# The prompt's second gate multiplied onto expert rows in the rounds instead of onto the final tiles

## The reference, cut to what matters

```
def run_trunk(x, c, ...):
    sh1, sc1, gt1, sh2, sc2, gt2 = jnp.split(mod[:, None, :], 6, axis=-1)
    ...
    h = rmsnorm(x, p['g_norm_ffn'][l]) * (1.0 + sc2) + sh2
    x = x + gt2 * hier_moe(h, l, p)
    ...
    y = rmsnorm(x, p['g_final'])

def hier_moe(h, l, p):      # every row goes to 2 of 32 experts
    for e in range(N_EXPERTS):
        hid = jax.nn.silu(x @ p['w_exp_gate'][l, e]) * (x @ p['w_exp_up'][l, e])
        out = out + combine[:, e:e + 1] * (hid @ p['w_exp_down'][l, e])
```

## Time and profile before

| | |
|---|---|
| median of 3 runs | 1513.41 us (1513.18 to 1515.0) |
| the profiled execution | 1518.33 us, span from first to last instruction 1516.6 us |
| busy PE, DVE, ACT, POOL | 1367.9, 532.2, 284.2, 125.8 us |
| rounds | 1147 to 1437 us of the span |
| loop, one turn | 1438 to 1457 us |
| gathers and final tiles | 1463 to 1516.6 us |
| mean granted TensorE clock | 0.949 of full speed |

### The profile page before, as it was taken

How to read it: one execution, slowest core, us unless ns; L and a number is a source line. 1 busy time by engine, 2 the same in 40 slices (tenths; PEclk the granted TensorE clock), 3 DMA queues, 4 the chain that set the end, 5 groups by cost and what they waited for, 6 DMA issues and landing times. The chain is left out here.

```text
span 1516.6 us, 20884 instructions
## 1 busy us (share of the span) xinstructions
PE 1367.9 (90%) x8687; PEld 899.4 (59%) x8687; DVE 532.2 (35%) x1186; ACT 284.2 (19%) x666; POOL 125.8 (8%) x138
## 2 busy tenths in 40 slices
PE   4999999999999999998999999999967999999830
PEld 3565667888988666665567656689853333333210
DVE  4423222224433225780290224343752421111118
ACT  4100000003433310112322212121221111111103
POOL 0000000110020015001000000000001000000033
PEclk9799999999999989999999999999977999999965
DMA  9423422323441253232410355440055999999748
GB/s 311 143 84 124 134 83 92 104 82 118 166 179 53 74 148 122 76 130 74 84 57 10 121 161 172 162 148 28 29 218 208 361 378 415 418 416 415 300 126 245
DMA packets 132895, 256.55 MB, mean 169 GB/s; under 512 B 23191, under 2 KB 97575, under 8 KB 124585
## 3 DMA queue, kind: packets, MB, share of 16 engines
q1 hardware_dynamic: 106850, 192.29, 35.9%
q0 software_dynamic: 11264, 34.23, 6.9%
q10 hardware_dynamic: 14688, 28.71, 5.1%
HBM read 207.77 MB, written 50.17 MB: 170 GB/s over the span
## 5 line engine op out<-in xcount | busy, mean ns | idle before, releaser
L380 PE MATMUL psum<-h_t,ring 128*128 128x352 f32 x576 | 174.1, 464 | 2.7 <-DVE h_t L545 2.7
L380 PEld LDWEIGHTS psum<-h_t,ring 128*128 128x128 f32 x576 | 110.1, 192 | 65.6 <-issue 6.4
L1069 PE MATMUL psum<-h_t,ring 128*128 128x352 f32 x384 | 119.3, 469 | 3.2 <-PEq L667 3.2
L2137 PE MATMUL psum<-ring,big 128*128 128x256 f32 x512 | 116.7, 387 | 2.1 <-PEq L1819 2.1
L2137 PEld LDWEIGHTS psum<-ring,big 128*128 128x128 f32 x512 | 97.9, 194 | 16.3 <-issue 3.1
L2244 PE MATMUL psum<-w_gate_up,u_rows 128*32 128x512 f32 x608 | 100.3, 601 | 2.9 <-ACT u_rows L2365 1.1
L2244 PE MATMUL psum<-ring,u_rows 128*32 128x512 f32 x576 | 100.3, 596 | 0.9 <-ACT u_rows L2365 0.9
L1069 PEld LDWEIGHTS psum<-h_t,ring 128*128 128x128 f32 x384 | 73.4, 194 | 42.9 <-issue 5.6
L395 PE MATMUL psum<-ring,h_t 128*128 128x256 f32 x384 | 92.4, 397 | 0.0
L395 PEld LDWEIGHTS psum<-ring,h_t 128*128 128x128 f32 x384 | 85.5, 285 | 3.5 <-issue 0.4
L2266 PE MATMUL psum<-big 128*32 128x512 f32 x736 | 83.7, 595 | 0.8 <-DVE big L2676 0.8
(11 more groups left out here) (462 smaller groups left out, 1862.6 us busy)
## 6 DMA issues: line engine op xcount, KB each, us to landing
big<-in_w_exp_down SPq DMA_DIRECT2D x32, 1024.0 KB, 13.1
ring<-in_w_ada SPq DMA_DIRECT2D x24, 1024.0 KB, 7.2
w_gate_up<-in_w_exp_gate SPq DMA_DIRECT2D x13, 1024.0 KB
w_gate_up<-in_w_exp_up SPq DMA_DIRECT2D x13, 1024.0 KB
ring<-in_w_exp_gate SPq DMA_DIRECT2D x13, 1024.0 KB, 6.5
ring<-in_w_exp_up SPq DMA_DIRECT2D x13, 1024.0 KB, 8.6
tmp_expert_rows<-zero_rows POOLq DMA_DIRECT2D x12, 1024.0 KB
ring<-in_w_in SPq DMA_DIRECT2D x11, 1024.0 KB, 8.5
```

The lines of the kernel that those rows point to most:

```text
L380: m = nc.tensor.matmul(bank[(e + j) % NB][:, 0:CW], w[:, k, c * P:(c + 1) * P], ht3[:, k, j * CW:(j + 1) * CW], start=(k == 0), stop=(k == ...
L1069: m = T_.matmul(bank[4 + u % 4][:, 0:CW], w_[:, k, c0:c0 + P], ht3[:, k, j * CW:(j + 1) * CW], start=(k == 0), stop=(k == KT - 1))
L2137: m = T_.matmul(bank[2 * (i % 2) + b // 2][0:r, (b % 2) * WB:(b % 2 + 1) * WB], merged_t[:, k, t * P:t * P + r], w[:, k, :], start=(k == 0 ...
```

## The change

1. `copy_down` is DVE's alone. For each half it first builds `gate_of`, 128 x 512 (`gate_rows`: the prompt's gate where the row's token is a prompt token, one elsewhere), waits for it, and multiplies the bank by it on the way to `y_e`. That is four dependent instructions instead of one, and ACT's copy is gone.
2. On DVE `copy_hid(b)` now stands ahead of `copy_down(b - 1)`.
3. PE and ACT wait for DVE's semaphore alone.
4. The loop does the same: two flags, two gate halves, and two multiplications at its end.
5. In the final tiles the multiplication by `gate2` is left for the sample tile alone.
6. Three small instructions after routing and two in `overflow_map` make the flags of every slot (1 or 0 by the token's number). A few tiles move in SBUF.

```diff
                 def store(b):
-                    act.wait_ge(s_dna, b + 1)
                     act.wait_ge(s_dnd, b + 1)
...
                     if b + 1 < ROUNDS:
                         copy_x(b + 1)
                     if b >= 1:
-                        copy_down(b - 1)
                         store(b - 1)
...
+                c.step(dve, V.tensor_copy(tok_f[:, :], tok_i[:, :]))
+                c.step(dve, V.tensor_scalar(of_prompt[:, 0:ROUNDS], tok_f[:, :], float(SEQ), None, ALU.is_lt))
+                c.step(dve, V.tensor_scalar(of_sample[:, 0:ROUNDS], of_prompt[:, 0:ROUNDS], -1.0, 1.0, ALU.mult, ALU.add))
...
                     dve.wait_ge(s_dn, b + 1)
                     if b >= 2:
                         dve.wait_ge(s_yst[b % 2], 16 * (b // 2))
-                    V.tensor_copy(y_e[b % 2][:, 512:D], bank[5]).then_inc(s_dnd, 1)
+                    for f in range(2):
+                        gate_rows(b, f)
+                        m = V.tensor_tensor(y_e[b % 2][:, 512 * f:512 * (f + 1)], bank[4 + f], gate_of[:, :], ALU.mult)
+                        if f == 0:
+                            c.step(dve, m)
+                        else:
+                            m.then_inc(s_dnd, 1)
+
+                def gate_rows(b, f):
+
+                    c.step(dve, V.scalar_tensor_tensor(out=gate_of[:, :], in0=row_p["gate2"][:, 512 * f:512 * (f + 1)], scalar=of_prompt[:, b:b + 1],
+                                                       in1=of_sample[:, b:b + 1].to_broadcast([P, 512]), op0=ALU.mult, op1=ALU.add))
...
                 for b in range(ROUNDS):
                     hidden(b)
+                    copy_hid(b)
                     if b >= 1:
                         copy_down(b - 1)
-                    copy_hid(b)
...
                 with dve.Fori(0, turns) as n:
+                    V.tensor_copy(lflag[:, 0:1], of_prompt[:, bass.ds(n + ROUNDS, 1)]).then_inc(s_llw, 1)
+                    V.tensor_copy(lflag[:, 1:2], of_sample[:, bass.ds(n + ROUNDS, 1)]).then_inc(s_llw, 1)
+                    dve.wait_ge(s_llw, 2 * n + 2)
+                    for f in range(2):
+                        V.scalar_tensor_tensor(out=gate_loop[f], in0=row_p["gate2"][:, 512 * f:512 * (f + 1)], scalar=lflag[:, 0:1],
+                                               in1=lflag[:, 1:2].to_broadcast([P, 512]), op0=ALU.mult, op1=ALU.add).then_inc(s_lgate, 1)
...
-                    V.tensor_copy(ly[:, 512:D], bank[5]).then_inc(s_ldnd, 1)
+                    V.tensor_tensor(ly[:, 0:512], bank[4], gate_loop[0], ALU.mult)
+                    V.tensor_tensor(ly[:, 512:D], bank[5], gate_loop[1], ALU.mult).then_inc(s_ldnd, 1)
...
                         dve.wait_ge(s_both[t], 16)
-                        c.step(dve, V.tensor_tensor(a, a, (row_p if t < TT else row_s)["gate2"][0:r, :], ALU.mult))
+                        if t == TT:
+                            c.step(dve, V.tensor_tensor(a, a, row_s["gate2"][0:r, :], ALU.mult))
```

## The result

Six runs of the changed kernel had a median of 1525.3 us (1523.16 to 1526.96), six of the one before 1514.2 (1511.37 to 1517.65): a ratio of 1.0062, 95% interval 1.0049 to 1.0076. So it is slower, as forecast, but 1525.3 lies outside the range of 1515.5 to 1522.0, and 11.1 us is nearly twice the +5.7 of the sum.

What follows compares the result with a forecast made beforehand. Bounds: PE and weight loads in the rounds, then last copies, loop and gathers, finally DVE with DMA nearly level. 2.63 + 2.27 + 0.61 + 1.8 - 1.6 = +5.7 us on a 1513.4 median gave 1519.1, range 1515.5 to 1522.0.

Steps and rivals of the forecast that it cites:

- The mid rounds cost nothing: Rounds before the last: the longer copy_down, 2.96 us for 0.69, fits DVE's idle time and adds nothing.
- the rival of the rounds: Rounds: later stores meet other weight loads, PE's weight waits double or triple, +3 to +5 us, about 1522.5; chance 0.10.
- The last round, +4.9: Last round: down(22) starts 2.63 us later, and the bare copy_down(22) delays PE's loop entry by 2.27.
- The loop's end, +0.61: End of the loop: two multiplications on DVE where ACT had taken one half, the second starting 0.61 us later.
- The clock, +1.8: Half clock after PE's longer gaps: down(22) +1.5 us, loop's transposes +0.8, products -0.5; between -3 and +8.
- The tail, -1.6: Final tiles: fewer DVE multiplications, but gather landings limit the gain to 1.6 us, between -0.8 and -3.7.
- The rival by which POOL's gathers come earlier: Final tiles: less DVE work lets POOL issue gathers earlier, 2.6 us back, +3.1 in all, 1516.5; chance 0.12.

Runs made afterwards that it cites:

- e1: The kernel before, unchanged, run again as a control: 1516.17 us against 1515.43, ratio 0.9994.
- e12: Changed kernel with gates built a round ahead, loop's turn count read early, final norm's row loaded by ScalarE ahead of the last store: 0.9975 of before.
- e5: Kernel before with only the order changed, copy_hid(b) ahead of copy_down(b - 1) on DVE: 1.0003 of before.
- e6: Kernel before with the final tiles' eight multiplications by the prompt's gate left out, nothing added: 0.9985 of before.
- e7: Changed kernel with unread products in PE's gaps, three ahead of down(22), three behind it, one in the loop: 1.0012 of before.
- e11: The changed kernel, unchanged, measured a third time: 1522.16 us, 1.0036 of before.
- e10: Changed kernel with gates built a round ahead from round 7 and the loop's turn count read early by PE and ScalarE: 0.998 of before.

## Why the prediction was right in direction and too small

**The mid rounds cost nothing: right.** H alone says little: it lies between 1422.8 and 1433.5 in nine profiles with the new copies in some form (mean 1429.9) and between 1428.4 and 1433.3 in five with the old ones (mean 1430.8). But the rounds themselves can be timed, from the `turn_x(1)` that ends round 0 to H. These are the rows of `turn_x(1)` in before and in the changed kernel:

```profile
1158.69 1.12 PE L2223 MATMUL psum<-ident,big 128*128 128x128 f32 x8
...
1160.74 1.12 PE L2228 MATMUL psum<-ident,big 128*128 128x128 f32 x8
```

To H it is 272.67 us in before and 272.69 in e1, and 272.80, 272.74 and 272.77 in the three profiles of the changed kernel: 0.1 us for 22 rounds. The tightest round came out a little tighter than computed, and still harmless (changed kernel, timeline; `hidden(3)` and the `turn_hid(3)` that needs it):

```profile
1194.75 0.24 DVE L2651 TENSOR_SCALAR overflow_block<-overflow_block,w_top 128x25 f32<-128x25 f32 x1
1195.20 0.48 DVE L2666 SCALAR_TENSOR_TENSOR big<-big,weight_of_slot,psum 128x256 f32<-128x256 f32 x1 [0.21 <-DVE overflow_block L2651]
...
1198.72 0.44 PE L2258 MATMUL psum<-ident,big 128*128 128x128 f32 x2
```

3.0 us to spare, where 3.2 were computed. PE's waits for gate and up weights went from 2.4 us to 2.9 in the same two places; a third wait, which the prediction left out, went from 0.8 to 0.5. So the rival of the rounds falls.

**The last round, +4.9: right.** Measured 2.72 (forecast 2.63) for `down(22)`'s start, and 2.3 to 2.5 (2.27) for the loop's entry behind the last copy.

**The loop's end, +0.61: wrong in sign.** From the last of the loop's products of gate and up to POOL's first gather it was 12.19 and 12.06 us in before and e1, and is 11.80, 11.71 and 11.85 in the three profiles of the changed kernel: -0.3. The copy is longer, as computed, but the later store meets less of the norm row's load and lands a microsecond sooner (e12). I had costed a DMA as if it were alone.

**The clock, +1.8: too small.** This is the term that was mis-sized. `down(22)` lost 2.83, 1.70 and 1.70 us (taken: 1.5, after a discount of one third for the case that the clock holds; it fell in all three profiles). The transposes lost 0.8, as taken. The products I let win 0.5 against the 10.00 of the earlier trace rows, and here it depends on what one compares with. The kernel before itself shows 10.00 and 9.97, the changed one 9.71, 9.62 and 9.62: -0.3, and the term is 2.1 + 0.8 - 0.3 = +2.6. But e5 and e6, with the old copies too, show 8.77 and 7.13; against the mean of all four, 9.0, the term is 2.1 + 0.8 + 0.7 = +3.6. Four profiles can't say which is nearer. By the rule of the Trainium skill that the prediction names ("TensorE: Matmul & The Clock Gate", Part 1, What's actually happening) each lengthened gap speaks against the change; the 0.50 in the windows above and e7 agree.

**The tail, -1.6: right.** -1.5, and its cause as well: tile 7's second gather started 27.35 us after the first one and landed 14.0 later, before 26.80 and 14.2. So the rows arrive when they did. The rival by which POOL's gathers come earlier falls with it. By line, the accumulating gathers of the changed kernel

```profile
L2126 POOL DMA_INDIRECT big<-tmp_expert_rows,slot_i x9: 1535/1590/2270, 1478.2 to 1504.8; - x9
```

and of before

```profile
L2121 POOL DMA_INDIRECT big<-tmp_expert_rows,slot_i x9: 1460/1544/2372, 1467.9 to 1493.9; - x9
```

take as long as ever, though DVE has eight instructions with two SBUF inputs less. The rule of the Trainium skill on the shared port pair ("SBUF — State Buffer", Who interferes with whom) may hold, but the removed instructions were not what made gathers long.

**The sum.** 2.7 + 2.3 - 0.3 + 2.6 - 1.5 = +5.8 us, or +6.8 with the larger clock term. The stretches after H of the three changed profiles and of before and e1 differ by 5.7 us in the mean (87.0 against 81.3), and the later comparisons gave 6.2 and 5.7. So the forecast of +5.7 was near what the change costs, with errors on both sides that partly cancelled: the loop's end 0.9 too high, the clock 0.8 or more too low.

**The first 1525.3.** It lies 6.2 us over the forecast of 1519.1. 2.4 of these are the base: three runs gave 1513.41, while the 128 later runs of the kernel before have a median of 1515.8, spread from 1505.6 to 1523.1. Another 0.4 is between the median difference of 24 later runs of the changed kernel (1521.9 - 1515.8 = 6.1) and 5.7. The remaining 3.4 lie between the first six runs of the changed kernel and these 24.

Most of that is the clock again, in a place where the sum put it at nothing. The mean granted clock was measured in every run. Over the 128 runs of before, the time falls by 1.2 us for each 0.001 of it (correlation -0.95), and over the 24 of the changed kernel by 1.1 (-0.94). The first six had a mean clock of 0.9463, the 24 one of 0.9485: 2.2 steps, about 2.5 of the 3.4 us. The profiled one of the six took 4.7 us more than that of e11, 3.2 of it in front of H and 1.5 behind. The traces say what makes H early or late. For each of the 14 profiles, take windows of 10 us from the start to H and add up (1 - clock) x length, the time that the granted clock took away. This sum runs from 34.0 us (e12, H 1422.78) to 47.8 (the changed kernel's first profile, H 1433.54), with 46.2 in before and 42.6 in e1. H follows it with a correlation of 0.99, 0.8 us for each us. One such place is round 0, here in the changed kernel and in e12:

```profile
1140.00:1160.00 20.00, 13.16 (x80) 5.51 (x80) 0.80 (x5) 2.31 (x2) 3.15 (x3) 0.59 0.52 186
...
1140.00:1160.00 20.00, 18.72 (x145) 6.24 (x146) 5.60 (x21) 3.44 (x5) 2.00 (x2) 0.86 0.68 257
```

This code is the same in all these kernels but for a few small instructions on DVE, and both kernels show early and late H, so nothing here makes it a cost of the change. Why the clock returns sooner in one execution than in another stays open.

So the step of the prediction that failed is the clock: +1.8 for the last round and the loop, where the rows give 2.6 to 3.6, and nothing for its spread between executions, mostly in the stretch in front, by which the first six runs came out about another 2.5 us longer. A range of 1515.5 to 1522.0 around a median of three runs had no room for that. What the change itself costs, and by which instructions, was foreseen rightly but for the loop's end.

## What to carry to other kernels

Work that is free in every pass of a pipeline is bare in its last one: price the drain apart, with the consumer's gap and what the gap does to the clock, and build whatever does not depend on the awaited result ahead of the wait. 5.0 us of stall in front of TensorE cost 2.6 to 3.6 us of clock on top here, and seven unread products gave that part back (e7). Against a spread of several us between executions, three or six runs are no base for an effect of 0.4%; a fixed mark in the trace from which all stretches are counted is a better one, and the granted clock of each run tells how much of a difference is the clock's.

## What the runs showed of the hardware that I had not expected

Two 512 KB transfers issued 0.67 us apart, one a load and one a store, made the store land in 4.9 to 5.1 us; 1.35 us apart it was 3.7 to 4.0; alone 2.6 (e12, one profile). From the end of DVE's last copy to the loop's transposes PE took 1.3 us in before and 1.5 in the changed kernel, and 0.35 in e10, where it reads the loop's turn count ahead of the wait. The clock's share differed between executions: the same sixteen entries of products took from 7.13 to 10.00 us in kernels with the old copies. Over 128 executions of one program the time ranged over 17.6 us and followed the mean granted clock, 1.2 us for each 0.001.
